# A layer kernel on eight cores: the gMLP value chains are put into the same planned schedule as the RG-LRU chains

## What is computed

```
hn = rmsnorm(x);  z = hn @ w_in            # columns: gate_a | xa | u | v, 512 each
xa_c = causal_dwconv(xa, width 4)
r, i = sigmoid(block_diag(xa_c, w_r)), sigmoid(block_diag(xa_c, w_i))
a = exp(-8 r softplus(-lam));  h[t] = a[t] h[t-1] + sqrt(1 - a^2) * i * xa_c
ya = rmsnorm(h * gelu(gate_a))             # mixer A, RG-LRU
vn = layernorm(v)
yb = rmsnorm(u * (w_s @ vn + b_s))         # mixer B, gMLP, chunks of 128 positions
x  = x + rmsnorm(concat(ya, yb) @ w_o)
x  = x + rmsnorm(ffn(rmsnorm(x)))          # up, conv 3, GeGLU, down; phases B and C
```

## Time and profile before

| | |
|---|---|
| median of 3 runs | 1404.6 us (1404.54 to 1404.9) |
| the profiled execution, its own time | 1406.08 us |
| its span, slowest core (core 1) | 1405.0 us |
| spans of the eight cores | 1393.3 to 1405.0 us |
| granted TensorE clock, mean, by core | 0.816 to 0.829 |
| PE, DVE, ACT, POOL busy | 954.7, 693.0, 581.2, 245.8 us |
| activation table loads on ACT | 60, of 1.283 us each |

### The profile page before, as it was taken

One profiled execution on the slowest core, in us unless ns is written; L12 is line 12 of the kernel. 1 busy time (PEld: TensorE's weight loads), 2 busy tenths in 40 slices (PEclk: granted clock), 3 DMA queues, 4 the chain that ended last, 5 costly groups with the idle time before them and its releaser, 6 DMA issues.

```text
span 1405.0 us, 18756 instructions; the slowest of 8 cores (1393.3 to 1405.0 us)
## 1 busy us (share of the span) xinstructions
PE 954.7 (68%) x5828; PEld 536.0 (38%) x5828; DVE 693.0 (49%) x1475; ACT 581.2 (41%) x1084; POOL 245.8 (17%) x301
## 2 busy tenths in 40 slices
PE   1636764653379999989926275536424999998997
PEld 0212331222156666634412133212212666665443
DVE  3244644454347777731123446444532777777111
ACT  2272437336235555521113733453361555555111
POOL 5000000000034443322220000000000344333122
PEclk9965666675589999999967577757655999999999
DMA  9800000000056653201177000000003566331011
GB/s 210 158 0 1 1 0 0 1 0 1 4 95 123 124 94 64 46 16 46 60 153 161 0 1 1 0 0 0 1 1 58 94 123 120 62 62 31 30 45 58
DMA packets 21746, 71.94 MB, mean 51 GB/s; under 512 B 4368, under 2 KB 4752, under 8 KB 21520
## 3 DMA queue, kind: packets, MB, share of 16 engines
q0 software_dynamic: 15984, 50.60, 21.2%
q1 hardware_dynamic: 5664, 20.14, 4.1%
HBM read 111.99 MB, written 9.35 MB: 86 GB/s over the span
## 4 chain that ended last, share of the span: by engine, by line
PE 35%; DVE 23%; ACT 16%; issue 15%; DMA 7%; POOL 2%; DVEq 1%; ACTq 1%; POOLq 0%
PE bank L841 14%; DVE sb_arena L812 9%; ACT sb_arena L806 5%; PE bank L712 4%; PE bank L793 4%; PE bank L611 3%; DMA sb_rowb<-b_s 3%; PE bank L447 3%; PE bank L484 3%; DMA sb_r<-w_in 3%; DVE sb_arena L518 2%; DVE sb_arena L572 2%; DVE sb_x L737 1%; ACT sb_arena L437 1%; DVE sb_arena L732 1%
## 5 line engine op out<-in xcount | busy, mean ns | idle before, releaser
L793 PE MATMUL bank<-sb_hn2T,sb_arena 128*128 128x343 bf16 (+1 forms) x2304 | 365.4, 312 | 16.1 <-DMA sb_arena<-w_up 16.1
L812 DVE SCALAR_TENSOR_TENSOR sb_arena<-bank,sb_cst,sb_arena 128x407 f32<-128x407 f32 (+2 forms) x576 | 309.7, 592 | 113.7 <-ACT sb_arena L806 111.4
L793 PEld LDWEIGHTS bank<-sb_hn2T,sb_arena 128*128 128x128 bf16 x2304 | 219.4, 100 | 119.0 <-issue 16.4
L841 PE MATMUL bank<-sb_r,sb_arena 128*128 128x512 bf16 (+1 forms) x864 | 192.1, 386 | 10.4 <-DVE sb_osm L818 10.4
L826 POOL TENSOR_TENSOR sb_arena<-sb_arena 128x342 bf16<-128x342 f32 x144 | 137.7, 956 | 269.9 <-ACT sb_arena L824 165.2
L806 ACT ACTIVATE sb_arena<-bank,sb_cst 128x407 f32<-128x407 f32 (+2 forms) x288 | 170.9, 643 | 29.5 <-PE bank L793 29.5
L447 PE MATMUL bank<-sb_ident,sb_arena 128*128 128x128 f32 (+1 forms) x288 | 61.9, 388 | 172.7 <-DVE sb_arena L441 172.5
L133 POOL DMA_DIRECT2D sb_arena<-w_up x48 | 28.1, 586 | 727.3 <-DVE sb_hn2T L455 727.3
L824 ACT ACTIVATE sb_arena<-sb_arena 128x342 f32<-128x342 f32 x144 | 73.0, 507 | 185.1 <-DVE sb_arena L812 185.1
L484 PE MATMUL bank<-sb_arena,sb_r 128*128 128x512 bf16 (+1 forms) x576 | 118.8, 376 | 25.7 <-ACT sb_arena L489 11.3
L841 PEld LDWEIGHTS bank<-sb_r,sb_arena 128*128 128x128 bf16 (+1 forms) x864 | 86.7, 101 | 115.1 <-issue 18.1
(11 more groups left out here) (118 smaller groups left out, 993.8 us busy)
## 6 DMA issues: line engine op xcount, KB each, us to landing
sb_arena<-w_up POOLq DMA_DIRECT2D x48, 512.0 KB, 5.3
sb_r<-w_down POOLq DMA_DIRECT2D x24, 512.0 KB, 7.5
sb_r<-w_in POOLq DMA_DIRECT2D x16, 512.0 KB, 24.7
sb_x<-x SPq DMA_DIRECT2D x16, 512.0 KB, 28.1
y<-sb_x SPq DMA_DIRECT2D x16, 512.0 KB, 2.6
sb_r<-w_o POOLq DMA_DIRECT2D x8, 512.0 KB, 46.9
sb_bc<-bc SPq DMA_DIRECT2D x1, 1536.0 KB, 10.2
sb_x<-x SPq DMA_DIRECT2D x2, 256.0 KB, 42.6
```

Of the source, the lines that this page charges most:

```text
L793: S.op("pe", lambda e, bk=bk, kt=kt, half=half: e.matmul(bk[:, 0:n + 2], lhsT=wup[slot][:, kt, half * 128:(half + 1) * 128], rhs=hn2T[:, k ...
L812: S.op("dve", lambda e, bk=bk, acc=acc, tap=tap, cc=cc: e.scalar_tensor_tensor(out=acc[:, 0:nq], in0=bk[:, tap:tap + nq], scalar=w3(tap, c ...
L841: S.op("pe", lambda e, bk=bk, c=c, nh=nh: e.matmul(B[bk][:rows, :], lhsT=gT[:, c, c0:c0 + rows], rhs=wdn_sb[:, c, nh * 512:(nh + 1) * 512] ...
```

## The change

The four `ch3` chains are cut in two (`ch3a` up to the small matmuls, `ch3b` from the products with u on) and put into the same list as `chz` and `ch2a`. `ch3b(s)` waits for `ch3a(s)` and for `chz(3)`, since it reads u of all four column tiles; `ch3a(s)` waits for `ch3b(s-2)`. To free banks 7 and 1 for the v chains, each `ch2a` chain now has one bank (5 or 6) in place of two, so its w_i matmul comes after the tanh of the w_r matmul. A v chain uses one bank in place of two. The buffers vnb, sqb and vn get memory outside that of the A part. `colsum_setup` becomes a chain of the first stage's list with a ready time of its own (25 us in the planner's clock), and the v chains of that stage wait for it.

```diff
-                zb = (5, 6) if ci == 0 else (7, 1)
+                zb = 5 if ci == 0 else 6
...
-                S.op("pe", lambda e: e.matmul(B[zb[0]][:, 0:N], lhsT=wr_bd[:, ct, :], rhs=Q["xcb"][:, 0:N], start=True,
-                S.op("pe", lambda e: e.matmul(B[zb[1]][:, 0:N], lhsT=wi_bd[:, ct, :], rhs=Q["xcb"][:, 0:N], start=True,
-                yield
-                S.op("act", lambda e: e.activation(out=Q["rr"][:, 0:N], in_=B[zb[0]][:, 0:N], func=AF.Tanh, scale=0.5,
-                yield
-                S.op("act", lambda e: e.activation(out=Q["ii"][:, 0:N], in_=B[zb[1]][:, 0:N], func=AF.Tanh, scale=0.5,
+                S.op("pe", lambda e: e.matmul(B[zb][:, 0:N], lhsT=wr_bd[:, ct, :], rhs=Q["xcb"][:, 0:N], start=True,
+                yield
+                S.op("act", lambda e: e.activation(out=Q["rr"][:, 0:N], in_=B[zb][:, 0:N], func=AF.Tanh, scale=0.5,
+                yield
+                S.op("pe", lambda e: e.matmul(B[zb][:, 0:N], lhsT=wi_bd[:, ct, :], rhs=Q["xcb"][:, 0:N], start=True,
+                yield
+                S.op("act", lambda e: e.activation(out=Q["ii"][:, 0:N], in_=B[zb][:, 0:N], func=AF.Tanh, scale=0.5,
...
-            run_dag(dag)
-            S.fence(TP_KEYS, S2_KEYS)
-            if h == 0 and st == 0:
-                colsum_setup()
-
-            def ch3(s, ci):
+            def ch3a(s, ci):
                 c0 = s * 128
-                T = TP[ci]
-                vb, sbk = (2, 3) if ci == 0 else (4, 5)
+                T = dict(M3[ci], vn=vnS)
+                vb = sbk = 7 if ci == 0 else 1
...
-            run_window([(lambda s=s: ch3(s, s % 2)) for s in range(nsub)], lag=7)
+            dag = []
+            for ct in range(4):
+                dag.append(((lambda ct=ct: chz(ct)), [2 * ct - 2] if ct > 0 else []))
+                dag.append(((lambda ct=ct: ch2a(ct, ct % 2)), [2 * ct] + ([2 * ct - 3] if ct >= 2 else [])))
+            first = (h == 0 and st == 0)
+            for s_ in range(nsub):
+                dag.append(((lambda s_=s_: ch3a(s_, s_ % 2)),
+                            ([9 + 2 * (s_ - 2)] if s_ >= 2 else []) + ([8 + 2 * nsub] if first else [])))
+                dag.append(((lambda s_=s_: ch3b(s_, s_ % 2)), [8 + 2 * s_, 6]))
+            if first:
+                def cs_chain():
+                    colsum_setup()
+                    yield
+                dag.append((cs_chain, [], max(S.eng_free.values()) + 25.0))
+            run_dag(dag)
+            S.fence(TP_KEYS, S2_KEYS)
```

More of the change, by code:

```diff
@@ L256, in _build @@
                        sqa=ca.take([128, 512], BF16)))
+    M3 = []
+    for ci in range(2):
+        M3.append(dict(vnb=ca.take([128, 512], BF16), sqb=ca.take([128, 4, 128], BF16)))
+    vnS = ca.take([128, 512], F32)
     ct_ = Carve(split)
     TP = []
-    for ci in range(3):
-        TP.append(dict(xn=ct_.take([128, D], F32), junk=ct_.take([128, D], BF16), vn=ct_.take([128, 512], F32),
-                       vnb=ct_.take([128, 512], BF16), tmpA=ct_.take([128, 512], F32), mix=ct_.take([128, D], F32),
-                       sqb=ct_.take([128, 4, 128], BF16)))
+    for ci in range(2):
+        TP.append(dict(xn=ct_.take([128, D], F32), junk=ct_.take([128, D], BF16), tmpA=ct_.take([128, 512], F32),
+                       mix=ct_.take([128, D], F32)))
+    TP.append(dict(xn=ct_.take([128, D], F32), junk=ct_.take([128, D], BF16)))
     S2_KEYS = ["gg%d" % c for c in range(4)] + ["xa%d" % c for c in range(4)] + \
               [n + str(ci) for ci in range(2) for n in ("xc", "xcb", "rr", "ii", "aa", "hbuf", "sqa")]
-    TP_KEYS = [n + str(ci) for ci in range(3) for n in ("xn", "junk", "vn", "vnb", "tmpA", "mix", "sqb")]
+    TP_KEYS = [n + str(ci) for ci in range(3) for n in ("xn", "junk", "tmpA", "mix")]
+    M3_KEYS = ["vnb0", "vnb1", "sqb0", "sqb1", "vnS"]
     SH_KEYS = ["hnT%d" % s for s in range(4)] + ["u_sb"] + ["yTa%d" % c for c in range(4)] + ["yTb%d" % c for c in range(4)]
@@ L322, in run_dag @@
                 if state[k] is None and all(state[a_] == "done" for a_ in chains[k][1]):
-                    ch = {"gen": chains[k][0](), "ready": 0.0, "done": False, "pending": []}
+                    ch = {"gen": chains[k][0](), "ready": chains[k][2] if len(chains[k]) > 2 else 0.0, "done": False,
+                          "pending": []}
                     pull(ch)
@@ L528, in ch2a @@
                 yield
[L529 to L532 removed]
+                S.op("pe", lambda e: e.matmul(B[zb][:, 0:N], lhsT=wr_bd[:, ct, :], rhs=Q["xcb"][:, 0:N], start=True,
+                                              stop=True), r=["wr_bd", "xcb%d" % ci], w=["B%d" % zb])
                 yield
[L534 to L535 removed]
+                S.op("act", lambda e: e.activation(out=Q["rr"][:, 0:N], in_=B[zb][:, 0:N], func=AF.Tanh, scale=0.5,
+                                                   bias=clam[:, 8 + ct:9 + ct]), r=["B%d" % zb, "clam"], w=["rr%d" % ci],
+                     aset="t")
                 yield
[L537 to L538 removed]
+                S.op("pe", lambda e: e.matmul(B[zb][:, 0:N], lhsT=wi_bd[:, ct, :], rhs=Q["xcb"][:, 0:N], start=True,
+                                              stop=True), r=["wi_bd", "xcb%d" % ci], w=["B%d" % zb])
+                yield
+                S.op("act", lambda e: e.activation(out=Q["ii"][:, 0:N], in_=B[zb][:, 0:N], func=AF.Tanh, scale=0.5,
+                                                   bias=clam[:, 12 + ct:13 + ct]), r=["B%d" % zb, "clam"], w=["ii%d" % ci],
+                     aset="t")
                 yield
@@ L594, in ch2b @@
                 yield
-            dag = []
-            for ct in range(4):
-                dag.append(((lambda ct=ct: chz(ct)), [2 * ct - 2] if ct > 0 else []))
-                dag.append(((lambda ct=ct: ch2a(ct, ct % 2)), [2 * ct] + ([2 * ct - 3] if ct >= 2 else [])))
-            run_dag(dag)
-            S.fence(TP_KEYS, S2_KEYS)
-            if h == 0 and st == 0:
-                colsum_setup()
-            def ch3(s, ci):
+            def ch3a(s, ci):
                 c0 = s * 128
-                T = TP[ci]
-                vb, sbk = (2, 3) if ci == 0 else (4, 5)
+                T = dict(M3[ci], vn=vnS)
+                vb = sbk = 7 if ci == 0 else 1
                 kv, ks = "B%d" % vb, "B%d" % sbk
@@ L638, in ch3 @@
                                                          in1=bc[:rows, BC_BV:BC_BV + 512], op=ALU.add),
-                         r=["vn%d" % ci, "bc"], w=["vn%d" % ci])
+                         r=["vnS", "bc"], w=["vnS"])
                     yield
                     S.op("act", lambda e: e.activation(out=T["vnb"][:rows, :], in_=T["vn"][:rows, :], func=AF.Copy),
-                         r=["vn%d" % ci], w=["vnb%d" % ci])
-                    S.dma("sp", "vns", vns_d[h, :, :], T["vn"][:rows, :], r=["vn%d" % ci])
+                         r=["vnS"], w=["vnb%d" % ci])
+                    S.dma("sp", "vns", vns_d[h, :, :], T["vn"][:rows, :], r=["vnS"])
                     yield
@@ L675, in ch3, with ch3b @@
                     yield
-                    gsc = lambda hd: gvgob[:, hd:hd + 1]
+            def ch3b(s, ci):
+                c0 = s * 128
+                T = M3[ci]
+                sbk = 7 if ci == 0 else 1
+                ks = "B%d" % sbk
+                gsc = (lambda hd: C("gob", 1, hd)) if isS else (lambda hd: gvgob[:, hd:hd + 1])
                 for hd in range(4):
```

11 lines of the change are left out of this document (3 added, 8 removed).

## The result

The changed kernel took **1418.6 us** (median of 8 runs, 1416.0 to 1419.4) against 1404.6 for the kernel before in the same session (median of 8). The ratio is 1.010, 95% interval 1.0089 to 1.0112: slower, inside the range, 3.6 us above the forecast of 1415. Executions in which one die ran at a lower clock are left out of the ratios.

A forecast was written before the change was run, and what follows sets the result against it. Chains hopping between PE, ACT and DVE, and queue order, were taken to bound main stages' parts. 3 x 1.0 + 1.3 + 3.4 + 2.4 = +10.1 us on the median of 1404.6 gave 1414.7, rounded 1415; range 1399 to 1431.

The forecast's parts named there:

- The trade: In a main stage the A part grows by 16.0 us and the v tail shrinks by 15.0.
- the three places with one load: Where tanh behind a square root is followed by exp, one table load serves both; otherwise 3.8 us more.
- Its milestones: Second main stage, after its first projection matmul: first tanh at 19.9 us, first square 35.5, last square 75.7.
- The main stages' +1.0: Each of three later main stages, first projection matmul to reduction, gets 1.0 us longer.
- 1.7 us for a set of small matmuls: In a main stage's v tail, each set of small matmuls takes 1.7 us, within a tail of 10.8.
- The first stage: Last square 17.6 us later, as PE waits for a weight at the colsum matmuls; tail 16.3 shorter: +1.3 us.
- The sample stages: Last square 16.5 us later, tail 13.1 shorter: +3.4 us, and +2.4 in the second, whose first matmuls may run faster.
- The projection behind the mixer: Its order is the same, so its granted clock was taken as unchanged and it was left out of the sum.
- the shared bank costs nothing here: At the second tanh of a main stage's first A chain, w_i's matmul is long done: no cost.
- The rival "faster": v work fits in ACT's idle time: 37 us less, 1368; needs under 15 us of main-stage A delay; chance 0.15.
- The 2.66 of the Trainium skill: Table load priced with its drain, in place of 1.28 us: 16 added loads cost 22 us more, time 1437.
- The rule of the Trainium skill on interleaving: Where the busiest engine changes over time, interleaving can improve the time; it pointed towards 1368 us.

The follow-up runs named there:

- p2: The changed kernel with each chain's two gate matmuls and two tanh kept as one piece on banks 5 and 6; 1415.3 us.
- r1: The kernel before with only the split pair: one bank per ch2a chain, w_i's matmul behind w_r's tanh, no overlap; 1425.8 us.
- p1: The kernel before with each chain's two gate matmuls and two tanh as one piece on banks 5 and 6; 1400.7 us.
- r6: The changed kernel with the square root of the v chains' layernorm replaced by Identity; 1402.9 us.
- p5: p2 with the v chains of main stages let in only behind the last projection chain, colsum behind the second; 1395.8 us.
- b1: The changed kernel, pair whole, v pieces counted 3 us later, main stages' v chains and colsum behind all A chains (only sample stages overlap); 1421.7 us.
- b2: b1 with two banks for each v chain of a main stage, run by `run_window` with a lag of 7 as before; 1389.9 us.
- r3: The changed kernel with the v chains of main stages let in only behind the last projection chain; 1426.7 us.
- r4: The changed kernel with the first stage's colsum chain let in only behind the second projection chain; 1415.6 us.

## Why the prediction was right, point by point

**The trade** held: longer A part, shorter tail, nearly even. Against the kernel before on the same core (core 5), whose start ran at the same clock, the first tanh came 5.1 us later (forecast 5.2), the first square 9.6 (9.6), the last 16.1 (16.0). Loads: 76, as counted, so the three places with one load were read rightly.

**Its milestones** were some 3 us late throughout: first tanh at 16.7 for 19.9, first square 32.3 for 35.5, last 72.7 for 75.7. They were laid over a core whose projection matmuls had run slower in that stage: 48 took 14.38 us on core 1, at a granted clock of 0.60 in the first 6 us, and 11.28 on core 5, at 0.87. The first tanh stood at 14.7 and 11.6; of the eight only core 0, with 14.0, was like core 1. The differences don't suffer from it, the absolute marks do.

**The main stages' +1.0** was mis-sized: they measured +1.7, +2.4 and +2.3. The A parts grew by 15.8, 16.2 and 16.4 us, for 16.0; most of the error is the tail, 10.8 by the forecast and 11.8 by the rows (269.98 to 281.75). I took 1.7 us for a set of small matmuls; in that stretch the granted clock is 0.50, and a set begins at 271.42 and the products that read it at 273.75, 2.3 us, and so again from 276.44 to 278.76.

**The first stage** measured +2.4 for +1.3: the A part +17.1 for +17.6, the tail 14.7 shorter for 16.3. PE waits at the colsum matmuls as forecast. **The sample stages** measured +1.9 and +2.9 for +3.4 and +2.4; in the first of them the first square came at 21.6 for 22.6, the last at 43.2 for 45.0 (core 5). The reason for taking less in the second came out the other way: its value matmuls (L611) took 3.12 us there and 2.76 in the first on that core, for 3.5 in the forecast. The two stages together measured +4.8 for +5.8. Sum: +13.7 for +10.1, so the errors partly cancel: the mains and the first stage were 4.5 too low, the samples 1.0 too high. The projection behind the mixer kept its clock as taken: its matmuls last 468 ns each, before 470.

**The step that failed, though the sum didn't show it,** is "the shared bank costs nothing here". It is right for the one place of which it was said, L545 in a main stage. But p2 against the change shows that the split, with the order that the planner then makes, costs 6 us in each sample stage, and r1 shows 2.4 to 3.4 us in every kind of stage without overlap. In the change that loss hides a gain: with the pair whole, overlap makes a sample stage 4 us shorter (42.5 to 38.4), with the pair split 1 us (45.4 to 44.4). The costs of split and overlap don't simply add. By the six stages together the split alone took 19.0 us (435.4 to 454.4, r1), and overlap then gave back 5.3 (449.1, the change); with the pair whole, overlap took 14.6 (431.6 in p1 to 446.2 in p2), and the split 2.9 more. That the forecast missed this and was still near is in part luck: it laid out the changed order as it stood and counted four more loads in a sample stage, of which two go with the split (13 for 11), so the price was partly in the sum under another name.

**Where the expected gain went.** In a main stage the v pieces stood ahead of A pieces on DVE and ACT. The rival "faster" needed less than 15 us of delay to the A chains, and it was 16. Three of these 16 are two table loads ahead of the first tanh. Ten such loads in the later main and the sample stages are worth the whole loss: without them (r6) the kernel takes 0.998 of the time before. Price of a load: two cost 2.84 us in the timeline and 3.0 to 3.1 in the stage's length, so 1.4 to 1.5 each. The 2.66 of the Trainium skill (ScalarE: Activation LUTs, What ACT_TABLE_LOAD costs) would have made it 5.3. The rule of the Trainium skill on interleaving (Perfetto Trace Analysis, Optimization Strategy, the section behind the one that the prediction names), which says only that it may help, holds for the sample stages once the pair is whole, but not for the main stages: two orders with the pair whole gave 91.2 and 89.5 for p1's 84.5 without overlap, and the third, with hardly any overlap left in it, 84.7 (p5). With the pair split, overlap took 1 us off a main stage (88.8 to 87.7), which is less than the splitting put on.

**What stays open.** b1 against b2 changed two things, the banks of a v chain and who orders them, so which made the long tail isn't settled. One bank for each v chain doesn't make it in every order: p5 has b1's banks and tails of 26 to 27 us, with the value matmuls of its first two v chains ahead of the last A square. That main stages can't gain from overlap is shown for the orders tried, not for all. r3's first stage, 6 us above the change's, was not taken apart. How much of r4's 3 us is the place of the colsum matmuls is open too.

## What to carry to other kernels

Chains that hop between engines are bound by their hand-overs; before filling the idle time of an engine, look at what each filled-in piece stands ahead of, and count a table load on either side of it. A resource that is freed to make overlap possible (here a bank, by splitting a pair of matmuls) has to be priced in the kernel without overlap first: here it cost 19 us, and the overlap gave back 5. And try an overlap stage by stage, since here it took 6 us off each small stage and gave nothing in the large ones in the orders tried.

## What the runs showed of the hardware

In the profiled executions the cores' mean granted clock was 0.819 to 0.828 in the changed kernel and 0.834 to 0.840 in b2, with the same 5828 matmuls. Within one main stage of the changed kernel (core 5), 24 projection matmuls took 5.82 us at a granted clock of 0.92 (from 197.27), and 24 more 7.92 us at 0.67 (from 220.32). Ahead of the second 24 PE had waited 4.81 us for ACT, up to the w_r matmul at 219.94. So a gap that an order leaves in front of PE can be paid for a second time; no run here changes that gap alone.
